# Four orders in a four-layer transformer kernel: the last blocks of the down product, the pool stage, input splits and mixer queues

## The reference, cut to what matters

```python
for i in range(2):
    h = h + mixer_i(rms_norm(h, norm_mix[i]))           # A: blocked causal attention, B: latent (MLA) attention
    h = h + conv_ffn(rms_norm(h, norm_ffn[i]), ...)     # F0, F1 (gelu)
h = rms_norm(h, norm_final)
h = h + pool_mixer(rmsnorm(h, mix_norm_2[0]))           # POOL: trailing means minus h, linear map per group
h = h + conv_ffn_2(rmsnorm(h, ffn_norm_2[0]), ...)      # F2 (silu)
h = h + chunk_attention(rmsnorm(h, mix_norm_2[1]))      # DD: attention with head norms and a relative bias
h = h + conv_ffn_2(rmsnorm(h, ffn_norm_2[1]), ...)      # F3 (silu)

def conv_ffn(xn, w_gate, conv_w, conv_b, w_up, w_down):
    g = xn @ w_gate
    gc = conv_b + sum(conv_w[j] * shift(g, j) for j in range(3))
    return (gelu(gc) * (xn @ w_up)) @ w_down            # 1024 -> 2816 -> 1024
```

## Time and profile before

| what | us |
|---|---|
| median of 3 runs (1116.78 to 1120.87) | 1117.85 |
| the profiled execution | 1117.43 |
| its span, first to last instruction | 1115.6 |
| TensorE busy | 1091.6 (98%) |
| VectorE busy | 851.4 (76%) |
| ScalarE busy | 656.1 (59%) |
| DMA | 191.74 MB, mean 172 GB/s |

### The profile page before, as it was taken

One profiled execution on the slowest core, in us unless ns is written; L12 is line 12 of the kernel. 1 busy time (PEld: TensorE's weight loads), 2 busy tenths in 40 slices (PEclk: granted clock), 3 DMA queues, 4 the chain that ended last, 5 costly groups with the idle time before them and its releaser, 6 DMA issues.

```text
span 1115.6 us, 17454 instructions
## 1 busy us (share of the span) xinstructions
PE 1091.6 (98%) x7166; PEld 975.9 (87%) x7166; DVE 851.4 (76%) x1247; ACT 656.1 (59%) x925; POOL 1.3 (0%) x8
## 2 busy tenths in 40 slices
PE   7989999999999999999999999999999999999998
PEld 7988988888898798888888888888899989888888
DVE  6877589886567768988766899885649767998851
ACT  6466457664447655766555587654457754876540
POOL 0000000000000000000000000000000000000000
PEclk9999999999999999999999999999999999999999
DMA  8443246645435144664554166555554432665540
GB/s 326 152 161 141 77 151 229 225 174 209 160 136 183 41 152 161 227 210 178 208 189 177 39 226 226 189 193 199 195 177 170 143 114 113 226 227 189 197 153 29
DMA packets 31375, 191.74 MB, mean 172 GB/s; under 512 B 4416, under 2 KB 5568, under 8 KB 11328
## 3 DMA queue, kind: packets, MB, share of 16 engines
q1 hardware_dynamic: 31296, 190.62, 48.2%
HBM read 189.56 MB, written 1.05 MB: 171 GB/s over the span
## 4 chain that ended last, share of the span: by engine, by line
PE 88%; DVE 6%; ACT 3%; issue 1%; DMA 1%; SPq 0%; DVEq 0%; ACTq 0%
PE banks L406 21%; PE TB L406 12%; PE banks L407 11%; PE SB L406 10%; PE banks L372 6%; PE TB L407 6%; PE banks L373 6%; PE banks L374 6%; PE SB L407 5%; DVE wlo L1450 1%; ACT whi L1018 1%; ACT sc L1102 1%; PE TB L519 1%; PE banks L539 1%; DMA raw<-in_a_qkv 1%
## 5 line engine op out<-in xcount | busy, mean ns | idle before, releaser
L1450 DVE TENSOR_TENSOR wlo<-raw,whi 128x2048 fp32r<-128x2048 f32 (+2 forms) x181 | 398.0, 2203 | 91.7 <-ACT whi L1018 91.7
L1018 ACT ACTIVATE whi<-raw 128x2048 fp32r<-128x2048 f32 (+2 forms) x181 | 332.1, 1839 | 84.2 <-PE banks L407 34.3
L406 PE MATMUL banks<-xx,whi 128*128 128x512 f32 x704 | 247.6, 394 | 0.0
L407 PE MATMUL banks<-xx,wlo 128*128 128x256 f32 x704 | 195.7, 278 | 0.0
L406 PEld LDWEIGHTS banks<-xx,whi 128*128 128x128 f32 x704 | 131.9, 187 | 30.3
L406 PE MATMUL TB<-xx,whi 128*128 128x512 f32 x384 | 135.9, 394 | 1.0 <-DVE xx L1455 1.0
L407 PEld LDWEIGHTS banks<-xx,wlo 128*128 128x128 f32 x704 | 132.4, 188 | 0.1
L372 PE MATMUL banks<-whi,xx 128*128 128x256 f32 (+2 forms) x400 | 119.5, 299 | 9.6 <-DVE wlo L1919 7.5
L373 PE MATMUL banks<-wlo,xx 128*128 128x256 f32 (+2 forms) x400 | 116.3, 291 | 0.0
L374 PE MATMUL banks<-whi,xx 128*128 128x256 f32 (+2 forms) x400 | 116.2, 290 | 0.0
L406 PE MATMUL SB<-xx,whi 128*128 128x512 f32 x320 | 111.8, 393 | 0.0
(11 more groups left out here) (209 smaller groups left out, 2035.2 us busy)
## 6 DMA issues: line engine op xcount, KB each, us to landing
raw<-in_gate SPq DMA_DIRECT2D x44, 1024.0 KB, 4.8
raw<-in_up SPq DMA_DIRECT2D x44, 1024.0 KB, 4.8
raw<-in_down SPq DMA_DIRECT2D x32, 1024.0 KB, 4.7
raw<-in_down SPq DMA_DIRECT2D x16, 768.0 KB, 4.3
raw<-in_d_qkv SPq DMA_DIRECT2D x12, 1024.0 KB, 4.8
raw<-in_a_qkv SPq DMA_DIRECT2D x10, 1024.0 KB, 5.2
raw<-in_a_o SPq DMA_DIRECT2D x4, 1024.0 KB, 4.8
raw<-in_b_o SPq DMA_DIRECT2D x4, 1024.0 KB, 4.7
```

What stands on the lines that cost most here:

```text
L406: e.matmul(b[:, m, 0:512], wh[:, k, sl], both, start=start, stop=stop, skip_group_check=True)
L407: last = e.matmul(b[:, m, 0:256], wl[:, k, sl], a[:, kk, 0, :], start=False, stop=stop, skip_group_check=True)
L1018: e.activation(whi[n % RING][:, 0:nk * w], raw[n % RAW][:, 0:nk * w], ACT.Copy).then_inc(s_hi, 1)
L1450: e.tensor_tensor(wlo[n % RING][:, 0:nk * w], raw[n % RAW][:, 0:nk * w], whi[n % RING][:, 0:nk * w].bitcast(F32), ALU.subtract).then_inc(s ...
```

## The change

Six edits. (1) The last pair of every down product, `last_pair`: block 6 (m = 0) goes through all 22 k tiles first, in the wide form, then block 7 through all 22 with `three`. The three units are given back (`s_used`) in the second pass. A new semaphore `s_half` tells when block 6 is complete. Its residual (`residual_6`, semaphore `s_r6`) and block 7's (`residual_7`) are 128x256 each, and the next stage's input tiles 6 and 7 are prepared one by one (`last_input` on ACT), with hi(first+2) and hi(first+3) of the next stage between them on ACT, lo(u+36) ahead of residual_7 and lo(u+37) behind it on DVE. In F3 tiles 6 and 7 are stored one by one. (2) In `next_input` of every stage but POOL, both splits stand ahead of the squares, on ACT and DVE. (3) In the pool stage DVE norms pair g+1 and then adds pair g, in place of all eight tiles first. (4) In A, on ACT, hi(u+3g+7) stands ahead of exponentials(2g) for every g; it stood behind them for g = 0 and at the end of the group before for g = 1, 2. (5) In DD, on DVE, normalize(6) stands ahead of pair(7). (6) In B, on ACT, hi(u+13) and hi(u+14) stand at pairs 6 and 7.

```diff
@@ sync_program
-            for c in range(4):
+            for c in range(3):
                 e.wait_ge(s_res, n_res(F3, c))
                 e.dma_start(out[:, 2 * c:2 * c + 2, :], xT[:, 2 * c:2 * c + 2, :]).then_inc(s_out, 16)
-            e.wait_ge(s_out, 64)
+            e.wait_ge(s_r6, 4)
+            e.dma_start(out[:, 6, :], xT[:, 6, :]).then_inc(s_out, 16)
+            e.wait_ge(s_res, n_res(F3, 3))
+            e.dma_start(out[:, 7, :], xT[:, 7, :]).then_inc(s_out, 16)
+            e.wait_ge(s_out, 80)
@@ tensor_program
+            def block_wide(n, po, m, k, a, kk, start, stop):
+                wh, wl = unit(n)
+                sl = slice(m * 128, (m + 1) * 128)
+                e.matmul(po[:, 0:512], wh[:, k, sl], a[:, kk, :, :].rearrange("p w s -> p (w s)"), start=start,
+                         stop=stop, skip_group_check=True)
+                return e.matmul(po[:, 0:256], wl[:, k, sl], a[:, kk, 0, :], start=False, stop=stop,
+                                skip_group_check=True)
+            def last_pair(s):
+                b = ffn_banks(s, 5)
                 for m in range(2):
+                    kk = 0
+                    for n, nk in zip(range(first[s] + 31, first[s] + 34), (8, 8, 6)):
+                        wh, wl = unit(n)
+                        if m == 0:
+                            weights_here(n)
+                        for k in range(nk):
+                            start, stop = kk == 0, kk == NF - 1
+                            if m == 0:
+                                last = block_wide(n, b[:, 0, :], 0, k, hx, kk, start, stop)
+                            else:
+                                last = three(b[:, 1, 0:256], wh[:, k, 128:256], wl[:, k, 128:256], hx[:, kk, 0, :],
+                                             hx[:, kk, 1, :], start, stop)
+                            kk += 1
+                        if m == 1:
+                            last.then_inc(s_used, 1)
+                    if m == 0:
+                        last.then_inc(s_half, 1)
@@ scalar_program
             def next_input(s, c):
                 e.wait_ge(s_res, n_res(s - 1, c))
+                if s != POOL:
+                    split_x(s, 2 * c)
+                    split_x(s, 2 * c + 1)
                 squares(s, c)
                 if s == POOL and c < 3:
                     scaled_squares(c)
-                split_x(s, 2 * c)
-                split_x(s, 2 * c + 1)
+                if s == POOL:
+                    split_x(s, 2 * c)
+                    split_x(s, 2 * c + 1)
+            def last_input(s):
+                L = LAYER[s - 1]
+                e.wait_ge(s_add, n_add(s, 2))
+                for m in range(2):
+                    if m == 0:
+                        e.wait_ge(s_r6, L + 1)
+                    else:
+                        hi(first[s] + 2)
+                        hi(first[s] + 3)
+                        e.wait_ge(s_res, n_res(s - 1, 3))
+                    if s != POOL:
+                        split_x(s, 6 + m)
+                    last = e.activation(sq[:, m, :], xT[:, 6 + m, :], ACT.Square)
+                    if m == 1:
+                        last.then_inc(s_sq, 1)
+                    if s == POOL:
+                        split_x(s, 6 + m)
...
+                for q in range(9):
+                    hi(u + 22 + q + 5)
+                    if q % 3 == 2:
                         if s == F3 and q > 2:
                             e.wait_ge(s_res, n_res(s, q // 3 - 1))
                         e.wait_ge(s_used, u + 22 + q + 1)
+                        halves(q // 3)
                         if s != F3:
                             next_input(s + 1, q // 3)
+                if s == F3:
+                    e.wait_ge(s_res, n_res(s, 2))
+                e.wait_ge(s_half, L + 1)
+                halves(3)
+                if s != F3:
+                    last_input(s + 1)
+                    hi(u + 38)
@@ scalar_program, A
+                        hi(u + 3 * g + 7)
                         exponentials(s, j)
-                        if g == 0:
-                            hi(u + 7)
                         hi(u + 3 * (g + 1) + 5)
...
                         if g < 2:
                             value(g + 1)
-                            hi(u + 3 * (g + 1) + 7)
@@ scalar_program, B
-                    if j in (5, 6):
-                        hi(u + 8 + j)
+                    if j in (6, 7):
+                        hi(u + 7 + j)
@@ vector_program
+            def residual_6(s):
+                L = LAYER[s]
+                r = rtmp[:, 0, :]
+                e.wait_ge(s_rl, 4 * L + 4)
+                kept(e.tensor_tensor(r, ffn_banks(s, 5)[:, 0, 0:256], r, ALU.add))
+                after_own()
+                kept(e.tensor_tensor(r, r, rb[:, :], ALU.mult))
+                after_own()
+                e.tensor_tensor(xT[:, 6, :], r, xT[:, 6, :], ALU.add).then_inc(s_r6, 1)
+            def residual_7(s):
+                r = rtmp[:, 1, :]
+                e.wait_ge(s_res, n_res(s, 2))
+                e.wait_ge(s_used, first[s] + 34)
+                kept(e.tensor_tensor(r, ffn_banks(s, 5)[:, 1, 0:256], rb[:, :], ALU.mult))
+                after_own()
+                e.tensor_tensor(xT[:, 7, :], r, xT[:, 7, :], ALU.add).then_inc(s_res, 1)
...
+                residual_6(s)
+                if s != F3:
+                    split_x(s + 1, 6)
+                    lo(u + 36)
+                residual_7(s)
+                if s != F3:
+                    split_x(s + 1, 7)
+                    if s + 1 != POOL:
+                        add_squares(s + 1, 3)
+                    lo(u + 37)
@@ vector_program, DD
+                    normalize(s, 6)
                     pair(7)
-                    normalize(s, 6)
@@ vector_program, POOL
-                for k in range(KD):
-                    kept(e.scalar_tensor_tensor(out=xT[:, k, :], in0=xT[:, k, :], scalar=vcol("norm_final", k),
-                                                in1=rb[:, :], op0=ALU.mult, op1=ALU.mult))
+                def normed_pair(g):
+                    for k in (2 * g, 2 * g + 1):
+                        kept(e.scalar_tensor_tensor(out=xT[:, k, :], in0=xT[:, k, :], scalar=vcol("norm_final", k),
+                                                    in1=rb[:, :], op0=ALU.mult, op1=ALU.mult))
+                normed_pair(0)
                 for g in range(NG):
                     xp = xT[:, 2 * g:2 * g + 2, :]
+                    if g < 3:
+                        normed_pair(g + 1)
                     e.wait_ge(s_uu, g + 1)
-                    if g == 0:
-                        after_own()
+                    after_own()
                     e.tensor_tensor(xp, xp, pu[:, 2 * g:2 * g + 2, :], ALU.add).then_inc(s_res, 1)
```

More of the change, by code:

```diff
@@ L122, in build @@
         s_pad, s_ub, s_tap, s_conv = sem("s_pad"), sem("s_ub"), sem("s_tap"), sem("s_conv")
+        s_half, s_r6 = sem("s_half"), sem("s_r6")
         s_gr, s_sr, s_gl, s_ul, s_rl = sem("s_gr"), sem("s_sr"), sem("s_gl"), sem("s_ul"), sem("s_rl")
@@ L397, in across @@
                 return last
+            def block_wide(n, po, m, k, a, kk, start, stop):
[5 more added lines that the diff above has]
+                                skip_group_check=True)
             def across_wide(n, b, k, a, kk, start, stop):
-                wh, wl = unit(n)
-                both = a[:, kk, :, :].rearrange("p w s -> p (w s)")
+                block_wide(n, b[:, 0, :], 0, k, a, kk, start, stop)
+                return block_wide(n, b[:, 1, :], 1, k, a, kk, start, stop)
+            def last_pair(s):
+                b = ffn_banks(s, 5)
                 for m in range(2):
-                    sl = slice(m * 128, (m + 1) * 128)
-                    e.matmul(b[:, m, 0:512], wh[:, k, sl], both, start=start, stop=stop, skip_group_check=True)
-                    last = e.matmul(b[:, m, 0:256], wl[:, k, sl], a[:, kk, 0, :], start=False, stop=stop,
-                                    skip_group_check=True)
-                return last
+                    kk = 0
[15 more added lines that the diff above has]
+                        last.then_inc(s_half, 1)
             def along(n, po, h, a, kk, start=True):
@@ L481, in ffn @@
                     e.wait_ge((s_gr, s_ub)[c % 2], n_ff(s, 9 + c // 2))
+                    if c == 3:
+                        last_pair(s)
+                        break
                     k0 = 0
@@ L487, in ffn @@
                                 e.wait_ge(s_hl, n_ff(s, (k0 + k) // 2))
-                            if (s, c) == (F3, 3):
-                                last = across(n, b[:, 0, :], k, hx, k0 + k, k0 + k == 0, k0 + k == NF - 1)
-                            else:
-                                last = across_wide(n, b, k, hx, k0 + k, k0 + k == 0, k0 + k == NF - 1)
+                            last = across_wide(n, b, k, hx, k0 + k, k0 + k == 0, k0 + k == NF - 1)
                         last.then_inc(s_used, 1)
```

(33 more changed lines are left out.)

20 lines of the change are left out of this document (8 added, 12 removed).

## The result

| what | before | after |
|---|---|---|
| median, us (four runs each) | 1118.1 | 1104.64 (1104.04 to 1105.21) |
| ratio, with its 95% interval | | 0.9876 [0.9856, 0.9897] |
| the profiled execution | 1117.43 | 1104.08 |
| its span | 1115.6 | 1102.3 |
| idle time of TensorE behind its first matmul | 12.3 | 3.4 |

The account below looks back on a forecast made before the run. TensorE, busy 98% of the span, was taken as the bound, so only its idle time, clock and work count. The terms summed to -12.1: 1105.3 us for the profiled execution, 1105.7 for the median, range 1103.0 to 1110.5.

Parts of the forecast that it names:

- A, -5.2: First mixer: high halves ahead of exponentials remove stalls of 0.8 and 2.9 us and a low clock of 1.6; 5.2 taken.
- The last pair: Down product's end: block 6 completes early, removing waits; -1.5 into B, -2.0 into the pool stage, -0.5 into DD.
- The price of block 7, +0.9: In F0, F1 and F2 block 7 takes the form with three 256-column matmuls, costing 0.9 us.
- the thin cover of hi(u+37) and lo(u+36): Down product's end: both splits finish about when the product does, residual_7 late by at most 0.4; cost taken as nothing.
- rivals 3 and 4: 3: early half brings nothing, 1111.3, chance 0.07; 4: lo(u+37) holds the norm chain, 1123, chance 0.03.
- The clock at the pool sums, -1.6: Pool stage: the low clock behind the 2.0 us stall was expected to go with it, gaining 1.6 us.
- Pool stage pair by pair, -0.8: F2's first input: norming by pairs shortens TensorE's 1.0 us wait; 0.8 taken, bounds 0 and -1.0.
- B's tail, -0.7: Second mixer: hi(u+13) moved one pair on stands behind the copy of pt, removing a 0.7 us wait.
- DD, +0.5: Last mixer: the 1.1 us wait on sc goes but returns one step later through late exponentials(7); 0.5 us slower.
- The end, -1.2: Behind the last matmul: shorter DVE operations -0.5, smaller last store -0.4, with F3's 0.3; together -1.2 us.
- the straight line through 1024 KB and 256 KB: Last store: load and store landing times of 4.8 and 2.0 us imply 0.4 to 0.5 saved for 128 KB; -0.4 taken.
- rival 1: Pool stage: the clock falls at the narrow sum matmuls all the same, +1.6 us, 1107.3; chance 0.18.

Follow-up runs that it names:

- u+7 alone: Kernel before with one edit: in A, group 0, hi(u+7) ahead of the first exponentials on ACT; 1114.21 us.
- the second profile of the changed kernel: The changed kernel timed once more with nothing changed, its profiled execution having the low clock in the pool stage; median 1105.45 us.
- the last kernel: Changed kernel plus wide matmuls between pool sums and, in DD, pt(6) copied ahead of exponentials(7) and two k tiles at either place; 1102.15 us.

## Why the prediction was right, and where it was off

**A, -5.2: right in size, too simple in its mechanism.** The passage from the first scores to F0 became 5.3 us shorter, 5.1 with this edit alone. ACT's timeline of the changed kernel shows the move as predicted, the split in what had been ACT's idle time, and its landing in time:

```profile
38.46 1.92 ACT L1048 ACTIVATE whi<-raw 128x2048 fp32r<-128x2048 f32 x1 [3.30 <-DMA raw<-in_a_qkv]
42.27 0.40 ACT L1164 ACTIVATE sc<-sc,small 128x128 f32<-128x128 f32 x1 [1.90 <-DVE small L1710]
```

The prediction set 3.7 + 1.8 us against a stall of 2.9. But TensorE too comes to that place earlier, by the wait on nkq that has gone (0.8) and by the 0.3 at the first scores. With u+7 alone the copy came 3.0 us earlier (56.70 for 59.71) and TensorE 1.3 earlier (56.20 for 57.50), so only 1.7 of 2.85 closed, and the move of u+10 is needed for the rest. A share of the 1.5 for the clock is to be had only where the kernel before had lost it; in the execution profiled it had.

**The last pair: every wait named has gone.** Into B the waits on xx and cc (0.8 and 0.7), into the pool stage 2.0, into DD 0.5: all gone, and in the kernel with this edit alone as well. In time they gave more than was forecast, 1.9 for 1.5 in B and 0.7 for 0.5 in DD, by the overlap that a stall lays bare. The price of block 7, +0.9, is 3 x 0.28 = 0.84, and F3's is -0.3. No wait on whi or wlo shows in a down product, so the thin cover of hi(u+37) and lo(u+36) held, and rivals 3 and 4 did not come. That both splits stand ahead of the squares changed nothing at B and DD for pairs 0 to 2; no kernel undid it for the last pair.

**The clock at the pool sums, -1.6: half of it.** The forecast took the stall for its cause, with a chance of 0.18 that the clock falls all the same. It fell in 13 of 25 executions with no stall ahead, and in none of 8 with wide matmuls in between. The run of narrow matmuls was therefore enough without the stall, and the right chance was nearer one half. The price is 1.5. The Trainium skill (TensorE: Matmul & The Clock Gate, Part 1) calls the watch on activity free-running; two executions of one program, at 1.00 and at 0.50 in the same window, agree with it, and so do the two outcomes behind the same 2.85 us stall.

**Pool stage pair by pair, -0.8.** TensorE's wait of 1.0 went altogether. The prediction added what DVE saves and what ACT saves by the squares, 1.4, and took 0.8. Each part works alone, but they do not add: the squares alone (the second edit) close 0.5, DVE's order alone (the third) closes the whole, and the two together can't give more than the 1.0 that was waited.

**B's tail, -0.7.** The wait on pt is gone, and no other stands in B. No kernel took this edit alone, but the others are ruled out: the wait of 0.7 is there with the first or the fourth edit alone, and absent with the second, the third or the fifth undone. ACT's timeline of the changed kernel has the copy ahead of the split, where it stood behind it before:

```profile
389.75 0.81 ACT L1173 ACTIVATE pt<-TB 128x768 f32<-128x768 f32 x1 [0.42 <-PE TB L549]
390.46 1.91 ACT L1048 ACTIVATE whi<-raw 128x2048 fp32r<-128x2048 f32 x1
```

**DD, +0.5: right, by the step named.** ACT's and TensorE's timelines of the changed kernel:

```profile
894.42 0.40 ACT L1164 ACTIVATE sc<-sc,small 128x128 f32<-128x128 f32 x1 [3.73 <-DVE small L1710]
...
896.19 0.79 ACT L1173 ACTIVATE pt<-TB 128x768 f32<-128x768 f32 x1
```
```profile
897.03 0.43 PE L569 MATMUL banks<-pt,vv 128*64 128x128 f32 x2 [1.63 <-ACT pt L1173]
```

DVE's maxima of pair 7 come later, the exponentials start later and stand on ACT ahead of a copy whose input was there from some 894.0 on (the transposes start at 893.16 and take 0.82). 1.1 us of idle time removed and 1.6 added, 0.4 longer in the passage.

**The end, -1.2: 0.8.** DVE's two operations of 0.42 gave the 0.5, F3 the 0.3. The last store gave 0.1 and not 0.4: the profile's DMA groups of the changed kernel show the half-sized stores landing in hardly less time.

```profile
out<-xT SPq DMA_DIRECT2D x3, 256.0 KB, 2.0
out<-xT SPq DMA_DIRECT2D x2, 128.0 KB, 1.9
```

The step that failed is the straight line through 1024 KB and 256 KB, carried on to 128. The Trainium skill (DMA: Bandwidth & Descriptors, "Latency and other measured facts") was nearer, with most of a small transfer's time in the round trip.

**The sum.** 1105.3 was forecast for the profiled execution, which took 1104.08. By passages: B gave 0.7 more than forecast (2.9 for 2.2), DD 0.3 (0.3 for 0), the pool stage 0.3 (4.7 for 4.4) and A 0.1; ahead of the first scores and in the first wait there were 0.3 that no edit made; the end gave 0.4 less and F2 0.2 less. The term that was mis-sized is the price of a stall, taken as its listed idle time; it tells above all in B. For the median, half of the executions pay 1.5 us of low clock in the pool stage, which the forecast had only as its rival 1, and by chance the two errors stand against each other: 1104.64 for 1105.7. The forecast's own range, stated as 1104 to 1108, comes to 1103.5 to 1107.5 by the terms given with it; the measured time lies in either.

## What to carry to other kernels

When an operation is moved ahead on one engine, follow the result to the engine that hands it on: the fifth edit removed 1.1 us on DVE and paid 1.6 on ACT, because the copy that TensorE waited for stood behind exponentials which the move had made late; moved together with that copy and a filler it gains some 0.7 to 0.8 against the kernel without it, and with two fillers 1.7 (the passage DD takes 120.56 us in the last kernel, 122.24 with the edit undone). Stretches of very narrow matmuls are worth breaking up with wide ones that are ready anyway, for the steadiness of the time as much as for its median. Where two edits work on the same wait, undoing one of them shows only what the other leaves. And read an edit's worth from the passage that it touches, between two landmarks on the engine that sets the end: whole times of this kernel lie on steps 1.2 to 1.5 us apart, which is more than most of its edits are worth.

## What the runs showed of the hardware

- TensorE's granted clock fell to 0.50 (1.2 GHz) behind 24 narrow matmuls that followed wide ones without any idle time, in about half of the executions (in the second profile of the changed kernel it fell some 1.0 us behind the last of them, among wide ones), and it did not fall behind a stall of 2.85 us in one kernel where it had fallen in another. A stretch costs 1.5 us (15.79 against 14.30; 10.24 against 8.73); twice two of them followed each other.
- A stall can cost TensorE more than the idle time listed: 1.0 us or a little more for one of 0.84, since the matmuls around it lose their overlap. It was 0.2 for each of three stalls in B and less than 0.1 on average for four in A and the pool stage.
- A store of 128 KB lands in 1.9 us, one of 256 KB in 2.0.
- The wait for the first weights varies between 7.2 and 8.1 us over thirteen profiled executions, and with it where DVE's early work lies against TensorE's: the same wait on nkq was 0.8 us in one execution and 1.7 in two others.
